# A fused encoder layer: early loads into slots 2 to 5, a second projection half in quarters, and a router mask by match-and-replace

## The reference

```
h   = rmsnorm(x)
q, k, v, xr, yr, gates = split(h @ w_in + b_in)
A   = grouped attention(q, k, v) with rotary positions       # 8 query heads, 2 key heads
R   = (forward + backward gated linear recurrence of conv(xr)) * gelu(yr)
mix = sigmoid(g_A) * (A @ w_attn_o) + sigmoid(g_R) * (R @ w_lru_o)
x   = x + mix @ w_out                                        # "the projection" below
h   = rmsnorm(x)
top_val, top_idx = top_k(h @ w_router + b_router, 4)         # 32 experts
x   = x + sum over the 4 of softmax(top_val) * expert(h)     # clamped SwiGLU, 1024 -> 2 x 1024 -> 1024
out = rmsnorm(x)
```

## Time and profile before

| | us |
|---|---|
| median of 3 runs | 1136.55 (1136.1 to 1138.01) |
| the profiled execution | 1135.82 |
| its span | 1134.0 |
| TensorE busy in the span | 1082.5 (95%) |
| VectorE / ScalarE busy | 371.2 / 237.2 |
| bytes moved | 439.77 MB, mean 388 GB/s |
| mean granted TensorE clock | 0.989 of 2.4 GHz |

### The profile page before, as it was taken

One profiled execution on the slowest core, in us unless ns is written; L12 is line 12 of the kernel. 1 busy time (PEld: TensorE's weight loads), 2 busy tenths in 40 slices (PEclk: granted clock), 3 DMA queues, 4 the chain that ended last, 5 costly groups with the idle time before them and its releaser, 6 DMA issues.

```text
span 1134.0 us, 12887 instructions
## 1 busy us (share of the span) xinstructions
PE 1082.5 (95%) x5407; PEld 502.6 (44%) x5407; DVE 371.2 (33%) x645; ACT 237.2 (21%) x369; POOL 2.2 (0%) x10
## 2 busy tenths in 40 slices
PE   7999999999999999999998989898989899899987
PEld 7999899633333333333333333332333333333332
DVE  6997877522212222122121211111211212121212
ACT  5399961211111111111111110011110101010102
POOL 0000000000000000000000000000000000000000
PEclk9999999999999999999999999999999999999999
DMA  9544277999999999999999999999999999999996
GB/s 351 187 178 149 83 288 302 420 426 399 429 427 428 427 435 432 429 429 434 430 431 436 428 432 436 426 436 432 428 436 431 429 437 430 427 428 427 428 428 246
DMA packets 25636, 439.77 MB, mean 388 GB/s; under 512 B 3424, under 2 KB 4064, under 8 KB 6272
## 3 DMA queue, kind: packets, MB, share of 16 engines
q1 hardware_dynamic: 24976, 438.27, 91.5%
q10 hardware_dynamic: 624, 0.99, 0.2%
HBM read 438.20 MB, written 1.05 MB: 387 GB/s over the span
## 4 chain that ended last, share of the span: by engine, by line
PE 67%; DMA 28%; DVE 2%; SPq 1%; ACT 1%; issue 0%; DVEq 0%
PE ps L1493 26%; DMA slots<-in_w_down_dram 20%; PE ps L1175 13%; PE ps L1502 13%; DMA slots<-in_w_gu_dram 8%; PE ps L1457 5%; PE ps L1438 3%; PE ps L1551 2%; DVE slots_r L728 1%; SPq L406 1%; PE ps L1232 1%; PE ps L1452 1%; PE ps L1416 1%; PE ps L1528 0%; PE ps L1237 0%; PE ps L1277 0%
## 5 line engine op out<-in xcount | busy, mean ns | idle before, releaser
L1502 PE MATMUL ps<-slots,lru 128*64 128x512 f32 x1024 | 238.9, 608 | 17.2 <-DMA slots<-in_w_down_dram 17.2
L1493 PE MATMUL ps<-slots,lru 128*64 128x512 f32 x1024 | 227.7, 594 | 11.6 <-DMA slots<-in_w_gu_dram 11.0
L1493 PE MATMUL ps<-slots,qT 128*64 128x512 f32 x984 | 223.8, 596 | 5.9 <-DMA slots<-in_w_gu_dram 5.9
L1493 PEld LDWEIGHTS ps<-slots,lru 128*64 128x64 f32 x1024 | 74.1, 137 | 160.7 <-issue 139.7
L1493 PEld LDWEIGHTS ps<-slots,qT 128*64 128x64 f32 x984 | 68.9, 137 | 153.6 <-issue 145.7
L1502 PEld LDWEIGHTS ps<-slots,lru 128*64 128x64 f32 x1024 | 68.3, 138 | 142.2 <-issue 123.2
L1103 DVE COPY lru<-ps 128x512 f32<-128x512 f32 x32 | 22.1, 692 | 322.9 <-PE ps L1493 322.9
L1175 PE MATMUL ps<-slots_r 128*128 128x256 f32 (+1 forms) x812 | 107.7, 291 | 0.2 <-DVE slots_r L728 0.2
L1175 PEld LDWEIGHTS ps<-slots_r 128*128 128x128 f32 x812 | 102.2, 191 | 5.4 <-issue 2.5
L656 ACT ACTIVATE lru<-ps 128x512 f32<-128x512 f32 x32 | 19.1, 598 | 395.3 <-PE ps L1493 395.3
L1085 DVE TENSOR_SCALAR lru<-sq,rank_col,small 128x64 f32<-128x64 f32 x64 | 17.2, 312 | 242.8 <-PE ps L1438 242.8
(11 more groups left out here) (200 smaller groups left out, 648.6 us busy)
## 6 DMA issues: line engine op xcount, KB each, us to landing
slots<-in_w_gu_dram SPq DMA_DIRECT2D x40, 4096.0 KB, 29.2
slots<-in_w_gu_dram SPq DMA_DIRECT2D x44, 2048.0 KB, 18.8
slots<-in_w_down_dram SPq DMA_DIRECT2D x20, 4096.0 KB, 28.3
slots<-in_w_down_dram SPq DMA_DIRECT2D x22, 2048.0 KB, 20.7
slots<-in_pre_dram SPq DMA_DIRECT2D x13, 2048.0 KB, 8.6
slots<-in_w_down_dram SPq DMA_DIRECT2D x8, 512.0 KB, 31.0
slots<-in_pre_dram SPq DMA_DIRECT2D x3, 1024.0 KB, 7.1
slots<-in_w_gu_dram SPq DMA_DIRECT2D x3, 1024.0 KB, 17.5
```

Of the source, the lines that this page charges most:

```text
L1493: ins = nc.tensor.matmul(ps[64 * side:64 * side + 64, 4 + b, :], xgT[i % 2][:, k, :], rows[r][:, o:o + BANK], start=(k == 0), stop=(k == K ...
L1502: ins = nc.tensor.matmul(ps[64 * side:64 * side + 64, bank, :], actT[(i - 1) % 2][:, k, :], w[:, r, side * BANK:(side + 1) * BANK], start= ...
```

## The change

Line names in the text are those of the kernel before.

- The slot order changes from 2, 3, 6, 7, 0, 1, 4, 5 to 2, 3, 4, 5, 0, 1, 6, 7. Slots 4 and 5 are free after the sixth `branches`, and expert chunks 2 and 3 now go there at once.
- Chunk 14 moves from slots 4 and 5 to slot 6 and `late`, which are free after the eighth `branches`. It comes in four quarters of 512 KB (one row block c each) with a semaphore each, ScalarE rounds and VectorE subtracts it by quarters, and `mix_end(0)` waits for each row's low part. VectorE does its memsets ahead of these low parts.
- The chunk for `late` is loaded after those of slots 0, 1 and 6.
- ScalarE rounds the second half of chunk 11 before, not after, the last two merge gates.
- The transposes of token tile 1 are issued in two halves, the first ahead of tile 0's logits; ScalarE, not VectorE, copies it.
- The mask: the four largest logits and four huge numbers are handed to one match-and-replace over the logits padded by four huge numbers, and a compare gives the mask as bfloat16. Indices and the one-hot tile are made for both tiles at once, after the second ranks.
- `residual_in_bank(0)` moves behind `ranks(1)`; the gate matrix is transposed behind the first `gate_up` of expert 0.

```diff
-        SLOT_ORDER = [2, 3, LOWS, SLOTS - 1, 0, 1, 4, 5]
-        EARLIER = [5, 0, 4, 0, 5, 0, 1, 1]
-        FREED = {2: [(branch_ps, 3)], 0: [(mixed_ps, 1)], LOWS: [(branch_ps, KD)], 4: [(mixed_ps, 2)]}
+        SLOT_ORDER = [2, 3, 4, 5, 0, 1, LOWS, SLOTS - 1]
+        EARLIER = [5, 0, 4, 0, 4, 0, 1, 1]
+        FREED = {2: [(branch_ps, 3)], 4: [(branch_ps, 6)], 0: [(mixed_ps, 1)], LOWS: [(mixed_ps, 2)]}
-        PLACE = [2 * (c % PAIRS) for c in range(PRE - 3)] + [LOWS, 0, 4]
+        PLACE = [2 * (c % PAIRS) for c in range(PRE - 3)] + [LOWS, 0, LOWS]
...
                 elif c == 14:
                     sp.wait_ge(pv_ps, NQ // 2)
                     half_load(extra_rows(1, 0), EXTRA[1], 0, extra_full[1])
-                    half_load(wide[:, 0:2048], 3, 0, slot_full[SLOTS - 1])
-                    for k in range(2):
+                    half_load(wide[:, 0:2048], SLOTS - 1, 0, slot_full[SLOTS - 1])
+                    for k in range(4):
                         expert_load(k)
-                    sp.wait_ge(branch_ps, 6)
+                    sp.wait_ge(branch_ps, KD)
+                    for r in range(4):
+                        cs = slice(r * D, (r + 1) * D)
+                        sp.dma_start(whole(c)[:, cs], pre[c, :, cs]).then_inc(mix_in[r], 16)
+                    break
...
-            expert_load(2)
-            half_load(wide[:, 2048:], 3, 1, slot_full[SLOTS - 1])
+            half_load(wide[:, 2048:], SLOTS - 1, 1, slot_full[SLOTS - 1])
+            sp.wait_ge(merged_ok, KD)
+            half_load(extra_rows(1, 1), EXTRA[1], 1, extra_full[1])
+            for k in (4, 5, 6):
+                expert_load(k)
             n, j = step_of(EXTRA[0])
             sp.dma_start(late[:, :], expert_src(n, j)).then_inc(extra_full[0], 16)
-            for k in (4, 5):
-                expert_load(k)
-            sp.wait_ge(merged_ok, KD)
-            half_load(extra_rows(1, 1), EXTRA[1], 1, extra_full[1])
-            for k in RING_CHUNKS[6:SLOTS]:
-                expert_load(k)
...
             attention_high()
+            split_high(11, [1])
             group_pair(30)
-            split_high(11, [1])
             load_sqrt_table(2)
-            for c in range(12, PRE):
+            for c in range(12, PRE - 1):
                 split_high(c)
+            for r in range(4):
+                cs = slice(r * D, (r + 1) * D)
+                act.wait_ge(mix_in[r], 16)
+                nc.scalar.activation(high(PRE - 1)[:, cs], whole(PRE - 1)[:, cs], ACT.Copy).then_inc(split_hi, 1)
...
+            second_squares(0)
+            transposed_copy(2, 0, 1, 5)
+            root(2, slice(0, 1))
+            transposed_copy(3, 1, 0, 6)
+            second_squares(1)
+            transposed_copy(4, 1, 1, 5)
+            root(3, slice(1, 2))
...
+            def split_low_by_rows(c):
+                for r in range(4):
+                    cs = slice(r * D, (r + 1) * D)
+                    dve.wait_ge(split_hi, casts_before(c) + 1 + r)
+                    low_part(low(c)[:, cs], whole(c)[:, cs], high(c)[:, cs]).then_inc(mix_low, 1)
...
             def top_experts(t):
-                link(nc.vector.max_index(idx_u[:, t, :], top8[:, t, :], logit[:, t, :]))
-                link(nc.vector.tensor_copy(idx_f[:, t, :], idx_u[:, t, :]))
-                link(nc.vector.tensor_tensor(hot[:, t], slotno[:, 0:NE].unsqueeze(1).to_broadcast(four),
-                                             idx_f[:, t, 0:TOPK].unsqueeze(2).to_broadcast(four), ALU.is_equal))
-                link(nc.vector.tensor_reduce(mask[:, t, :], hot[:, t].rearrange("p k e -> p e k"), AX.X, ALU.add))
-                nc.vector.tensor_copy(mask_b[:, t, :], mask[:, t, :]).then_inc(mask_ok, 1)
+                link(nc.vector.tensor_copy(best[:, t, 0:TOPK], top8[:, t, 0:TOPK]))
+                link(nc.vector.match_replace(marked[:, t, :], best[:, t, :], padded[:, t, :], FOUND))
+                nc.vector.tensor_scalar(mask_b[:, t, :], marked[:, t, 0:NE], FOUND, None, ALU.is_ge).then_inc(mask_ok, 1)
                 nc.vector.tensor_scalar(nmax[:, t:t + 1], top8[:, t, 0:1], -1.0, None, ALU.mult).then_inc(top_ok, 1)
...
             def mix_end(n):
                 for c in range(4, KD):
+                    if n == 0:
+                        pe.wait_ge(mix_low, c - 3)
...
-            second_transposes(0)
+            second_transposes(0, 0)
+            second_transposes(0, 1)
             mix_end(3)
+            second_transposes(1, 0)
...
             logits(0, range(KD))
-            second_transposes(1)
-            residual_in_bank(0)
+            second_transposes(1, 1)
             logits(1, range(4))
...
                 gate_up(n, i, 0, single)
+                if first:
+                    pe.wait_ge(mask_ok, T + 1)
+                    for t in range(T):
+                        ins = nc.tensor.transpose(ps[0:NE, 6, t * P:(t + 1) * P], gate[:, t, :], ident)
+                    ins.then_inc(gateT_ps, 1)
...
             ranks(1)
+            residual_in_bank(0)
```

More of the change, by code:

```diff
@@ L48 @@
 FAR = 4096.0
+HUGE, FOUND = 1e38, 3e38
 WARM = 28
@@ L164, in encoder_layer @@
         hotg = tflat[:, 384:640].rearrange("p (t k e) -> p t k e", t=T, k=TOPK)
-        mask = tflat[:, 640:704].rearrange("p (t e) -> p t e", t=T)
         mask_b = tflat[:, 835:867].bitcast(bf16).rearrange("p (t e) -> p t e", t=T)
@@ L226, in encoder_layer @@
         fin_ok, zeros = sem("fin_ok"), sem("zeros_ok")
-        mix_part = sem("mix_part")
+        mix_part, mix_low = sem("mix_part"), sem("mix_weights_low")
+        mix_in = [sem(f"mix_weights_in{r}") for r in range(4)]
         last_in = [sem(f"last_quarter_in{r}") for r in range(8)]
@@ L738, in split_low @@
                 low_part(low(c), whole(c), high(c)).then_inc(split_lo, 1)
-            def split_low_by_halves(c):
-                w = WIDTH[c] // 2
-                for i in range(2):
-                    cs = slice(i * w, (i + 1) * w)
-                    dve.wait_ge(split_hi, casts_before(c) + 1 + i)
-                    ins = low_part(low(c)[:, cs], whole(c)[:, cs], high(c)[:, cs])
-                ins.then_inc(split_lo, 1)
+            def split_low_by_rows(c):
[3 more added lines that the diff above has]
+                    low_part(low(c)[:, cs], whole(c)[:, cs], high(c)[:, cs]).then_inc(mix_low, 1)
             lam = cst[:, C_LAM:C_LAM + 16]
@@ L984, in _ @@
             link(nc.vector.memset(rank_col[:, :, :], -1.0))
+            split_low_by_rows(14)
             def second_residual(n):
@@ L994, in second_residual, with transposed_copy @@
                                                op1=ALU.add).then_inc(x2_ok, 1)
-            def transposed_copy(t):
-                dve.wait_ge(tposed, KD + 2 * t + 1)
-                nc.vector.tensor_copy(x2T[:, t, 0:4, :].rearrange("p k n -> p (k n)"), ps[:, 4 + 2 * t, :]).then_inc(xT_v, 1)
-            four = [P, TOPK, NE]
+            def transposed_copy():
+                dve.wait_ge(tposed, KD + 1)
+                nc.vector.tensor_copy(x2T[:, 0, 0:4, :].rearrange("p k n -> p (k n)"), ps[:, 4, :]).then_inc(xT_v, 1)
+            four = [P, T, TOPK, NE]
             def top_values(t):
@@ L1020, in first_ranks @@
                 link(nc.vector.scalar_tensor_tensor(out=ranked[:, t, :], in0=ps[:, 4 + t, 0:NE], scalar=FAR,
-                                                    in1=mask[:, t, :], op0=ALU.add, op1=ALU.mult))
+                                                    in1=mask_b[:, t, :], op0=ALU.add, op1=ALU.mult))
                 link(nc.vector.tensor_scalar(rank_col[:, t, 0:NE], ranked[:, t, :], -FAR, None, ALU.add))
@@ L1027, in _ @@
                 second_residual(n)
-            transposed_copy(0)
+            transposed_copy()
             inverse_variance(ssum[:, 0:1], T + 1)
             second_residual(3)
+            nc.vector.memset(best[:, :, TOPK:], HUGE)
+            link(nc.vector.memset(padded[:, :, NE:], HUGE))
             dve.wait_ge(bias_in, 48)
             top_values(0)
-            transposed_copy(1)
+            top_experts(0)
             inverse_variance(ssum[:, 1:2], T + 2)
-            top_experts(0)
             first_ranks(0)
@@ L1041, in _ @@
             link(nc.vector.tensor_reduce(cmax, ps[0:1, 5, NE:2 * NE], AX.X, ALU.max))
+            expert_numbers()
             dve.wait_ge(ex_ok, T)
@@ L1379, in _, with second_transposes @@
                 mix(c)
-            def second_transposes(t):
-                pe.wait_ge(x2_ok, 2 * t + 2)
-                if t == 1:
+            def second_transposes(t, half_k):
+                pe.wait_ge(x2_ok, 2 * t + 1 + half_k)
+                if t == 1 and half_k == 1:
                     pe.wait_ge(xT_a, 1)
-                for k in range(KD):
-                    o = (k % 4) * P
-                    bank = 4 + 2 * t if k < 4 else 5
-                    ins = nc.tensor.transpose(ps[:, bank, o:o + P], x2[:, t, k * P:(k + 1) * P], ident)
-                    if k % 4 == 3:
```

(10 more changed lines are left out.)

31 lines of the change are left out of this document (20 added, 11 removed).

## The result

| | before | changed |
|---|---|---|
| median of 20 runs each, us | 1136.43 | 1138.4 |
| lowest to highest | 1135.65 to 1138.84 | 1136.57 to 1140.82 |
| ratio of the medians, 95% interval | | 1.0016 [1.001, 1.0022] |
| the profiled execution, its span | 1135.82, 1134.0 | 1140.42, 1138.6 |

The change made the kernel **slower by 2.0 us (0.16%)** where 0.3 us faster was forecast. That is less than the 0.2% that the text took as its limit, but the interval leaves out equality. The profiled execution is one of the slowest of its kernel (third of 20), so its pieces sum to more than the medians differ by. The executions of the kernel before fall into two groups, here 13 from 1135.65 to 1136.84 and 7 from 1137.54 to 1138.84, so a difference of medians under 1 us says little.

The account below looks back on a forecast made before the run. TensorE's progress to the issue at 272.12 was taken as the bound, the weight stream behind it. Terms -0.56 + 0.6 - 1.7 + 0.4 + 1.0 = -0.3 us gave 1136.3 us, range 1133.0 to 1139.5.

Parts of the forecast that it names:

- The lead of one chunk: Weight stream before chunk 8: runs 4.9 us ahead, then waits for TensorE to free slot 2; counted as 0 us.
- until the issue at 272.12, TensorE's own progress sets when the stream goes on: Experts 0 and 1: TensorE giving back slots releases the loads; only behind that issue is the stream alone the bound.
- stream rival: First experts: TensorE is no limit at 272, the stream stays ahead up to 4.9 us, about 1131.9; chance 0.15.
- ScalarE's order, -0.56: Projection, chunk 11: the merge comes sooner and TensorE's idle time before 162.85 goes, -0.56 us.
- Quarters, +0.6: Projection's end, chunk 14: last quarter lands at 199.4 if the four overlap, fourth low row late, +0.6 us, bounds 0 and +10.
- Late quarters: Chunk 14: small loads overlap only in pairs, the last lands some 4.4 us later, 1140.7 us; chance 0.13.
- Router, -1.7: Router up to expert 0's gather: masks sooner, gather starts 0.8 sooner and runs shorter; -1.7 us, bounds -0.8 and -2.3.
- That rival: Clock falls again, under the router's filled gap or expert 1's selection wait: 0.9 to 1.7 us at 1.2 GHz, 1137.7; chance 0.07.
- after 226: Sign that the forecast is wrong: the first expert product starts before 224 or after 226 us.
- Gate transposes and expert 1's selection, +0.4 and +1.0: Expert 0's first chunk: transposes now on TensorE's path, +0.4 us; VectorE's copy delays the selection expert 1's gather needs, +1.0 us.

Follow-up runs that it names:

- no_lead: The changed kernel with expert chunks 2 and 3 issued behind chunk 14's quarters instead of before them; 1138.69 us.
- loads_alone: The kernel before with only the new slot order, early chunks and chunk 14 in quarters; 1139.1 us.
- router_alone: The kernel before with only the change's router, residual product's place and gate transposes, loads and ScalarE's order as before; 1136.81 us.
- order_alone: The kernel before with only ScalarE's order changed, second half of chunk 11 before the last two merge gates; 1135.43 us.
- resid_back: The changed kernel with the first residual product back between the router products; 1138.86 us.
- gate_back: The changed kernel with the gate matrix transposed ahead of expert 0's first products again, as before; 1136.23 us.
- mask_again: The same kernel as mask_order, run again on another chip with its own runs of the kernel before; 1135.16 us.
- mask_order: The kernel before with ScalarE's order, the match-and-replace router and the later residual product; loads, chunk 14 and gate transposes as before; 1135.28 us.
- resid_early: mask_order with the residual product back between the router products; 1135.42 us.

## Why the prediction was wrong, step by step

**What bounds it: right for the change, too simple for its neighbours.** The lead of one chunk was worth nothing, and 1.89 us of TensorE's delay at chunk 16 were carried to the end. But "until the issue at 272.12, TensorE's own progress sets when the stream goes on" holds only while the stream is ahead of it. In no_lead TensorE was 1.6 us sooner at chunk 16 than before, and the stream 2.3 later. The bound is the later of the two. (Two readings of the forecast are off without changing this: a stretch before is under 0.9 busy, 268 to 271 us with 0.85 and 355 GB/s, behind the issue near 267, which speaks for its bound; and its stream rival's 4.9 us give 1131.7, not 1131.9.)

**ScalarE's order, -0.56: right, somewhat more.** From SyncE's issue near 154 us to the one near 191, both released by TensorE, it is 38.08 us in the three profiles with the old order (before, loads_alone, router_alone) and 37.30 in the other ten: -0.8. order_alone measured -1.2 in the medians, its interval -2.2 to -0.1.

**Quarters, +0.6: mis-sized, and the first step that failed.** From the release of the load behind `mix(3)` (198.30) to that behind `mix_end(3)` (212.36) it is 14.06 us in the changed kernel and 11.77 before: +2.3. The five profiles with quarters, all times but the last column in us behind the issue of the first quarter, from the trace:

| profile | first quarter in | last quarter in | mean of its 16 parts | fourth low row ready | from `mix(3)` to `mix_end(3)` |
|---|---|---|---|---|---|
| no_lead | 3.91 | 8.04 | 7.69 | 10.38 | 12.32 (+0.55) |
| loads_alone | 4.05 | 8.04 | 7.55 | 10.38 | 12.35 (+0.58) |
| resid_back | 4.47 | 8.41 | 7.75 | 10.75 | 12.69 (+0.92) |
| changed | 6.03 | 9.80 | 7.92 | 12.14 | 14.06 (+2.29) |
| gate_back | 5.85 | 10.06 | 7.80 | 12.40 | 14.33 (+2.56) |

In all five the fourth row is ready 2.34 us behind the last landing (2.4 was counted), and the loss grows with it one for one. With the last quarter in after 8.04 us the loss is the +0.6 of the forecast. So the step that failed is "Issued at 191.2, the last quarter lands at 199.4 if the four overlap": the 8.2 us from issue to landing was taken from one load of one execution, and it was 9.8 in the changed kernel. gate_back tells the last quarter from the first, which came sooner than in the changed kernel although the loss was larger:

```profile
200.29 1.06 ACT L624 ACTIVATE late_r<-slots 128x1024 fp32r<-128x1024 f32 x1 [0.67 <-DMA slots<-in_pre_dram]
201.38 1.23 DVE L745 TENSOR_TENSOR slots_r<-slots,late_r 128x1024 fp32r<-128x1024 f32 x1 [0.50 <-ACT late_r L624]
```

ScalarE waits for the last quarter, VectorE for ScalarE. Each load comes over 16 DMA engines, and the quarter is in when the slowest has its part in: the mean of the 16 hardly moves (7.6 to 7.9), the slowest is 0.4 to 2.3 us behind it. Why it lags more in some executions isn't shown; whether the last quarter of a typical one lands nearer 8 us or 10 isn't known either. "Late quarters", the rival on the slower side, had the place right and both reason and size wrong: it let the loads overlap only in pairs and the last land 4.4 us later, while they did overlap, landing 1.2 to 1.3 us apart, and the last was 1.6 later.

**Router, -1.7: right in work, and the second step that failed in this execution.** From the issue behind `mix_end(3)` to k8 it is 18.12 us before. With the clock up it is 15.89 (gate_back, router_alone, no_lead, mask_again), -2.2, just inside the bound of -2.3. In the changed kernel's profile it is 17.82, -0.3, outside the bound of -0.8: the fall to 1.2 GHz, now 6.8 us long and over the router's products, ate 1.9. That rival had a chance of 0.07 and a price of 1.4. Of the twelve profiles other than before's five show such a fall, and gate_back, the same program up to that point as the changed kernel, does not. How often the other executions have it isn't known. The first expert product at 226.49 was the sign "after 226" that the text had named.

**Gate transposes and expert 1's selection, +0.4 and +1.0: right.** From k8 to k16 it is 42.3 us in every profile with the gate transposes in their old place and 43.8 in every one with them behind the first products: +1.55, of which 1.0 is the wait of the gather for VectorE.

**The sum** in the changed kernel's profile, at chunk 16: order -0.8, quarters +2.3, router -0.3, gate transposes and selection +1.55, together +2.8; the execution was 0.9 ahead at its start by chance, which leaves the 1.89 between 272.12 and 274.01. Of the 3.0 us between this and the forecast's -0.3, 1.7 are the quarters and 1.4 the router under its slow clock. On medians: loads +2.6, router with late gate transposes +0.3, order -1.2, together +1.7, against +2.0 of the change as a whole; each of these is uncertain by about 1. The median of the loads is more than their profile explains (+0.6 for its quarters and +0.7 for its longer fall of the clock), so how the 2.0 us of a typical execution divide stays open. Between the pieces not everything adds: mask_order and mask_again less order_alone leave the router -0.2 to -0.5, gate_back less loads_alone and order_alone leaves -1.6.

## What to carry to other kernels

A transfer issued sooner is worth what the stream lacks when the consumer frees the first slot, and nothing beyond; compute both times before moving loads. When one load is cut so that three engines can work on its pieces in turn, the pieces save the time of the helpers (3.5 us here), but the last piece still hangs on the last landing: take that landing from several loads and executions, not from one, since it varied by 2 us here while the work behind it didn't vary at all. And before moving work behind a product "where it is free", list what stands behind it on the engine it hands its result to: here a copy of 0.4 us pushed a selection into the path for 1.0.

## What the runs showed of the hardware

**The end hangs on the slowest of 16 DMA engines.** Each load raises its semaphore 16 times. In the chain of before (first) and of mask_again the last chunk's issue and length are nearly the same,

```profile
1101.91 20.44 DMA slots<-in_w_down_dram
```

```profile
1101.68 20.39 DMA slots<-in_w_down_dram
```

yet stretches show the bytes of mask_again in 2 us sooner, before's first:

```profile
1117.00:1120.00 3.00, 3.00 (x16) 0.96 (x14) 0.00 (x0) 1.69 (x3) 0.00 (x0) 1.00 0.87 347
```

```profile
1117.00:1120.00 3.00, 3.00 (x18) 1.00 (x14) 0.00 (x0) 1.49 (x2) 0.00 (x0) 1.00 0.42 171
```

The 16 landings of the last weight load, from the trace, in us:

| profile | mean of 16 | the slowest, later by | span |
|---|---|---|---|
| before | 1120.78 | 1.57 | 1134.0 |
| changed | 1123.41 | 3.25 | 1138.6 |
| gate_back | 1120.65 | 3.05 | 1135.4 |
| no_lead | 1123.09 | 1.46 | 1136.3 |
| mask_again | 1118.59 | 3.48 | 1133.8 |
| resid_early | 1118.07 | 1.68 | 1131.4 |

In all thirteen profiles the span ends 11.7 to 12.0 us behind the slowest landing. Of the 4.6 us between the two spans of the table's first rows 2.6 are the stream, which is the change, 1.7 the slowest engine, 0.3 the closing work. (The Trainium skill, DMA: Bandwidth & Descriptors, the section on why a semaphore counts to 16, has each engine post its own part when its data are in; the landings agree.) The spread between first and last of the 16 grows in steps. From 285 us on the thirteen profiles hold fifteen steps of 1 us or more, each 2.2 to 8.1 us behind the start of a 16 KB transfer of the instruction queue, which takes 1.0 to 1.1 us of an engine, and none of them lies between 523 and 1004 us, where no such transfer is. Most such transfers (13 in a profile) leave the spread as it is. That they cause the steps is read from these times and wasn't tried; the kernel before had no step over 1 us in its profile, most others one or two, so a profile's span says less of a change than the mean landing does.

**The clock fell in some executions and not in others of the same kernel**: 6.8 us from 215.16 in mask_order, none there in mask_again. Neither the residual product's place nor the added products changed the time; the cause stays open.
